# The last quarter of a 256x1024 output closed in two halves on two more PSUM banks

## The reference

```python
h2 = rms_norm(x, ffn_norm_gain)
gate, up = jnp.split(jnp.einsum('bsd,df->bsf', h2, w_gate_up), 2, axis=-1)   # 2816 + 2816 columns
x = x + jnp.einsum('bsf,fd->bsd', jax.nn.silu(gate) * up, w_down)
...
y = x32 * lax.rsqrt(jnp.mean(x32 * x32, axis=-1, keepdims=True) + NORM_EPS)  # the final rms_norm
return (y * gain.astype(jnp.float32)).astype(x.dtype)
```

## Time and profile before

| | |
|---|---|
| median of 3 runs | 873.07 us (872.86 to 874.38) |
| the profiled execution's own time | 873.15 us |
| its span in the trace | 871.3 us |
| TensorE busy | 858.6 us, 99% of the span |
| VectorE busy | 578.6 us, 66% |
| ScalarE busy | 441.0 us, 51% |
| GpSimd busy | 59.8 us, 7% |
| mean granted TensorE clock | 0.998 |

### The profile page before, as it was taken

How to read it: one execution, slowest core, us unless ns; L and a number is a source line. 1 busy time by engine, 2 the same in 40 slices (tenths; PEclk the granted TensorE clock), 3 DMA queues, 4 the chain that set the end, 5 groups by cost and what they waited for, 6 DMA issues and landing times.

```text
span 871.3 us, 13400 instructions
## 1 busy us (share of the span) xinstructions
PE 858.6 (99%) x5434; PEld 742.4 (85%) x5434; DVE 578.6 (66%) x872; ACT 441.0 (51%) x647; POOL 59.8 (7%) x90
## 2 busy tenths in 40 slices
PE   8999999999999999999999999999999999999997
PEld 6888999898899888888889999777888888888885
DVE  5785664654556656565686997876476777877544
ACT  6654434564355544544476652455644555555342
POOL 1000000000020110000020014303000100000000
PEclk9999999999999999999999999999999999999999
DMA  9757754355554555456747783412465665555541
GB/s 291 245 184 217 223 182 139 120 167 179 170 191 156 186 170 169 148 204 204 264 121 253 203 165 107 147 50 50 145 239 161 204 189 177 181 180 192 169 170 48
DMA packets 124771, 151.61 MB, mean 174 GB/s; under 512 B 15991, under 2 KB 87926, under 8 KB 124710
## 3 DMA queue, kind: packets, MB, share of 16 engines
q1 hardware_dynamic: 124426, 150.41, 54.8%
q10 hardware_dynamic: 220, 0.28, 0.1%
q0 software_dynamic: 64, 0.07, 0.0%
HBM read 148.63 MB, written 3.68 MB: 175 GB/s over the span
## 4 chain that ended last, share of the span: by engine, by line
PE 94%; DVE 2%; ACT 1%; SPq 1%; DMA 1%; issue 1%; POOLq 0%; POOL 0%; ACTq 0%; DVEq 0%
PE bank L526 20%; PE bank L528 20%; PE bank L527 20%; PE bank L1345 9%; PE bank L552 5%; PE bank L1346 5%; PE bank L553 3%; PE bank L984 1%; PE bank L744 1%; PE bank L822 1%; PE bank L724 1%; DMA ring<-in_w_in 1%; SPq L1426 1%; PE bank L1106 1%; DVE w_lo L2162 1%
## 5 line engine op out<-in xcount | busy, mean ns | idle before, releaser
L2162 DVE TENSOR_TENSOR w_lo<-ring,w_hi 128x2048 fp32r<-128x2048 f32 (+2 forms) x134 | 297.9, 2228 | 136.6 <-ACT w_hi L1552 136.3
L1552 ACT ACTIVATE w_hi<-ring 128x2048 fp32r<-128x2048 f32 (+2 forms) x134 | 248.9, 1860 | 100.9 <-PE bank L528 74.6
L1345 PE MATMUL bank<-h_both,w_hi 128*128 128x512 f32 x352 | 124.8, 399 | 0.2 <-issue 0.2
L526 PE MATMUL bank<-h_both,w_hi 128*128 128x256 f32 x424 | 122.4, 289 | 0.6 <-DVE w_lo L2162 0.6
L527 PE MATMUL bank<-h_both,w_hi 128*128 128x256 f32 x424 | 119.9, 283 | 0.0
L528 PE MATMUL bank<-h_both,w_lo 128*128 128x256 f32 x424 | 119.9, 283 | 0.0
L1346 PE MATMUL bank<-h_both,w_lo 128*128 128x256 f32 x352 | 98.8, 281 | 0.0
L526 PE MATMUL bank<-w_hi,h_both 128*128 128x512 f32 (+2 forms) x224 | 86.1, 384 | 0.0
L528 PE MATMUL bank<-w_hi,h_both 128*128 128x512 f32 (+2 forms) x224 | 84.1, 375 | 0.0
L527 PE MATMUL bank<-w_lo,h_both 128*128 128x512 f32 (+2 forms) x224 | 84.0, 375 | 0.0
L526 PEld LDWEIGHTS bank<-h_both,w_hi 128*128 128x128 f32 x424 | 81.2, 192 | 2.2 <-issue 1.1
(11 more groups left out here) (407 smaller groups left out, 1517.0 us busy)
## 6 DMA issues: line engine op xcount, KB each, us to landing
ring<-in_w_in SPq DMA_DIRECT2D x59, 1024.0 KB, 5.1
ring<-in_w_gate_up SPq DMA_DIRECT2D x44, 512.0 KB, 4.7
ring<-in_w_down SPq DMA_DIRECT2D x10, 1024.0 KB, 5.0
ring<-in_w_mem_kv SPq DMA_DIRECT2D x8, 1024.0 KB, 9.9
ring<-in_w_gla_out SPq DMA_DIRECT2D x4, 1024.0 KB, 5.0
ring<-in_w_x_out SPq DMA_DIRECT2D x4, 1024.0 KB, 5.3
ring<-in_w_dsa_out SPq DMA_DIRECT2D x4, 1024.0 KB, 5.3
ring<-in_w_o SPq DMA_DIRECT2D x4, 1024.0 KB, 5.0
```

The costliest lines, as they stand in the source:

```text
L526: mm(o, ah, bh, start=start, stop=False, skip_group_check=True)
L1345: mm(o[:, :], wh[:, k - k0, w], h_both[:, :, k, :], start=k == 0, stop=False, skip_group_check=True)
L1552: act(w_hi[:, k % NHI, at:m], ring[:, order.index(name) % NSLOT, at:m], ACT.Copy)\
L2162: tt_(w_lo[:, i, at:m], ring[:, i, at:m], w_hi[:, k % NHI, at:m].bitcast(F), ALU.subtract)\
```

## The change

TensorE now sums only the first 20 of 22 hidden tiles of the last quarter into the bank of `wd11`. The last two tiles are computed as two halves of 256 columns, each in a bank of its own (`wl0`, `wl1`), first all of `wl0` and then all of `wl1`. VectorE adds three banks instead of one to the residual: `wd11` (512 columns, which now holds a partial sum), then `wl0` and `wl1` (256 columns each), and multiplies each half by the gain. ScalarE squares the two halves one after the other into two sums, and GpSimd folds in the extra sum with one more instruction. The last scaling is cut differently: VectorE takes 640 columns and ScalarE 384, where both took 512, and the transfers follow that cut.

```diff
                         q = k // 4
                         if q not in weights:
                             weights[q] = split_unit(f"wd1{q}", 512)
-                        ins = three(o, (f_hi[:, k, s], f_lo[:, k, s]), [w[:, k % 4, :] for w in weights[q]], False, k == FT - 1)
+                        if t == 0 or k < 20:
+                            ins = three(o, (f_hi[:, k, s], f_lo[:, k, s]), [w[:, k % 4, :] for w in weights[q]], False,
+                                        k == (FT - 1 if t == 0 else 19))
                     done(f"wd1{t}", ins)
+                for half in range(2):
+                    bank, part = open_bank(f"wl{half}"), slice(256 * half, 256 * half + 256)
+                    for k in range(20, FT):
+                        ins = three(bank[:, 0:256], (f_hi[:, k, s], f_lo[:, k, s]), [w[:, k % 4, part] for w in weights[5]],
+                                    k == 20, k == FT - 1)
+                    done(f"wl{half}", ins)
...
-                    sp.dma_start(out[0, 128 * t:128 * t + 128, 512 * c:512 * c + 512], xn[:, t, 512 * c:512 * c + 512])\
-                        .then_inc(signal("out_done"), 16)
+                    columns = slice(512 * c, 512 * c + 512 + 128 * t)
+                    sp.dma_start(out[0, 128 * t:128 * t + 128, columns], xn[:, t, columns]).then_inc(signal("out_done"), 16)
...
-                    sc.wait_ge(*read(f"wd{c}{t}"))
-                    half_squares("o", xres[:, t, 512 * c:512 * c + 512], 0, c, t)
-            last = xn[:, 1, 512:1024]
+                    if (c, t) == (1, 1):
+                        sc.wait_ge(*read("wl0"))
+                        act(probT[:, 2, 0:256], xres[:, 1, 512:768], ACT.Square, accum_out=sumsq[:, 8:9])\
+                            .then_inc(signal("sumsq_o"), 1)
+                        sc.wait_ge(*read("wl1"))
+                        act(probT[:, 2, 256:512], xres[:, 1, 768:1024], ACT.Square, accum_out=sumsq[:, 3:4])\
+                            .then_inc(signal("sumsq_o"), 1)
+                    else:
+                        sc.wait_ge(*read(f"wd{c}{t}"))
+                        half_squares("o", xres[:, t, 512 * c:512 * c + 512], 0, c, t)
+            last = xn[:, 1, 640:1024]
             sc.wait_ge(signal("rstd_o"), 2)
-            sc.wait_ge(signal("last_gained"), 1)
+            sc.wait_ge(signal("last_gained"), 2)
...
-                    rsqrt_second(name, col, t, TT + t + 1)
+                    if (name, t) == ("o", 1):
+                        gp.wait_ge(signal("sumsq_o"), 4)
+                        step(nc.gpsimd.tensor_scalar(var[:, 1:2], sumsq[:, 8:9], 1 / D, var[:, 1:2], ALU.mult, ALU.add))
+                    rsqrt_second(name, col, t, TT + t + 1 + (name == "o" and t))
...
+            bank_ready("wd11")
+            stt(xres[:, 1, s], bank_of("wd11")[:, :], rstd[:, 7:8], xres[:, 1, s], ALU.mult, ALU.add).then_inc(reader("wd11"), 1)
+            ve.wait_ge(*read("wd11"))
+            for half in range(2):
+                v = slice(512 + 256 * half, 768 + 256 * half)
+                bank_ready(f"wl{half}")
+                stt(xres[:, 1, v], bank_of(f"wl{half}")[:, 0:256], rstd[:, 7:8], xres[:, 1, v], ALU.mult, ALU.add)\
+                    .then_inc(reader(f"wl{half}"), 1)
+                ve.wait_ge(*read(f"wl{half}"))
+                tt_(xn[:, 1, v], xres[:, 1, v], g_fin[:, v], ALU.mult).then_inc(signal("last_gained"), 1)
+            ve.wait_ge(signal("last_gained"), 2)
+            result(1)
```

More of the change, by code:

```diff
@@ L1992, in _ @@
                 for t in range(TT):
-                    sc.wait_ge(*read(f"wd{c}{t}"))
-                    half_squares("o", xres[:, t, 512 * c:512 * c + 512], 0, c, t)
-            last = xn[:, 1, 512:1024]
+                    if (c, t) == (1, 1):
[9 more added lines that the diff above has]
+            last = xn[:, 1, 640:1024]
             sc.wait_ge(signal("rstd_o"), 2)
-            sc.wait_ge(signal("last_gained"), 1)
+            sc.wait_ge(signal("last_gained"), 2)
             act(last, last, ACT.Copy, scale=rstd[:, 3:4]).then_inc(signal("last_result"), 1)
             sc.wait_ge(signal("last_result"), 1)
-            sc.dma_start(out[0, 128:256, 512:1024], last).then_inc(signal("out_done"), 16)
+            sc.dma_start(out[0, 128:256, 640:1024], last).then_inc(signal("out_done"), 16)
         @block.gpsimd
@@ L2917, in result @@
                 for c in range(2 - t):
-                    o = xn[:, t, 512 * c:512 * c + 512]
+                    o = xn[:, t, 512 * c:512 * c + 512 + 128 * t]
                     tsc(o, o, r, None, ALU.mult).then_inc(signal("result"), 1)
@@ L2923, in _ @@
                 for t in range(TT):
+                    if (c, t) == (1, 1):
+                        break
                     bank_ready(f"wd{c}{t}")
@@ L2928, in _ @@
                     ve.wait_ge(*read(f"wd{c}{t}"))
[L2929 to L2933, removed]
+                    step(tt_(xn[:, t, s], v, g_fin[:, s], ALU.mult))
                     if c == 1:
                         result(t)
+            bank_ready("wd11")
[10 more added lines that the diff above has]
+            result(1)
 def kernel(**inputs):
```

## The result

The changed kernel took 873.88 us (median of 20 runs, 873.17 to 875.66), the kernel before 872.88 (20 runs, 872.13 to 874.38): a ratio of 1.0014, 95% interval 1.0007 to 1.002. That is slower by 1.0 us, inside the 0.2% that I had called no change. The forecast was 873.8.

The account below looks back on a forecast made before the run. TensorE is busy 99% of the span, but the change works only on the 6.2 us relay after its last matmul. Adds +0.89, less what comes back, give +0.7: 873.15 + 0.7 = 873.85, less 0.08 for the median, 873.8 us; range 872.5 to 874.9.

Parts of the forecast that it names:

- VectorE's queue: In the last quarter, VectorE's adds and first gain queue behind the t = 0 scalings; last add ends +0.89 us later.
- the first rival: VectorE keeps up, `wl1`'s add starts when TensorE is done, and transfers start 0.36 us earlier: 872.7 us; chance 0.12.
- TensorE's part: At TensorE's end, twelve 256-column matmuls take 1.43 us instead of 1.36: +0.07 us, costing nothing behind VectorE.
- What comes back: Behind the last add, the narrower square saves 0.22 us; factor +0.67 late, ScalarE's scaling +0.56, VectorE's +0.74.
- the term: The change's whole predicted effect on the kernel's end: +0.7 us.
- The upper bound of 1.0: Top of the bounds on the whole effect, +0.35 to +1.0 us, from the adds and the transfer.
- The estimate of +0.6 from the Trainium skill: Whole effect if VectorE's 256-column steps are priced by (N + 151)/0.96 ns, 0.424 us each: +0.6 us.
- Slow transfers: Final transfers out with mixed row widths run at half rate, +1.5 us on top of +0.7: 875.3 us; chance 0.04.
- The third: Same queue on VectorE, but its cost hidden or halved by overlapping adds or the last gain: +0.2 us, 873.3; chance 0.10.

Follow-up runs that it names:

- e1: The change with three more 256-column matmuls at the end of `wl1`: 873.8 us, ratio 1.0015 to the kernel before.
- e2: The change with the first half's gain moved behind the add of `wl1` on VectorE: 873.33 us, ratio 1.0009 to the kernel before.
- e3: The change with VectorE's scalings of t = 0 moved behind the last gain: 872.99 us, ratio 1.0004 to the kernel before.
- e4: The change with halves over five hidden tiles, VectorE doing partial add, `wl0` add and first gain before the t = 0 scalings: 872.66 us, ratio 0.9997.
- e7: e4 with the last scaling and transfers cut at 512/512 columns: 872.45 us, ratio 0.9994 to the kernel before.
- e6: The kernel before with only the 640/384 cut of the last scaling and transfers: 872.91 us, ratio 0.9999.
- e10: The change run again unaltered (the repetition): 873.65 us, ratio 1.0007 to the kernel before.
- e8: e4 with the cut at 384 columns for VectorE and 640 for ScalarE: 872.69 us, ratio 1.0002 to the kernel before.
- e11: e7 run again unaltered: 872.86 us, ratio 0.9999 to the kernel before.

## Why the prediction was right

**VectorE's queue.** Right, and shown by moving it. Shifting by the 0.17 us that this execution started `wd10`'s add later, I had the adds at 864.82, 865.60 and 866.45, and they started at 864.83, 865.61 and 866.47. e1 (TensorE later: nothing), e2, e3 and e4 (something out of the queue ahead of the last add: it starts earlier by 0.47, 0.82 and 0.98) tell it from TensorE's end and from the new banks. Two figures under the first rival were wrong without touching the sum: VectorE has 1.6 us to do ahead of the last add, and 2.1 only up to its end; and the residual add takes 0.75, the "1.1 us of work" stands in no row.

**TensorE's part.** Twelve matmuls at 0.119, `wl1` full at 865.14 + 0.17 = 865.31; measured 865.33. Its +0.07 (measured 0.08) was hidden, as priced.

**What comes back.** The square: 0.42 instead of 0.63. GpSimd's additional instruction lay at 866.80 to 867.06, under the last square. The scaling: 0.62 instead of 0.72 on ScalarE, 0.55 instead of 0.49 on VectorE. All as worked out. Two handovers weren't, and cancel: the last square starts 0.03 after the add where it was 0.09, and GpSimd starts 0.17 after the sum where it was 0.10. The factor is there 0.7 late, forecast 0.67.

**The sum.** The tail grew by 0.88 (0.82 in the repetition), the term was +0.7, so it was 0.18 too small. 0.04 of that is the choice of 0.7 between 0.74 by the sync engine's issue and 0.56 by ScalarE's: the end followed the sync engine, whose issue moved from 868.24 to 869.24, 0.83 later against the `wd10` add. Most of the 0.09 between 0.74 and 0.83 is VectorE's last scaling, which started 0.10 after GpSimd's factor was written (868.56 to 868.66), where it was 0.04 before; for t = 0 it was 0.10 before as well (863.75 to 863.85), and what decides between the two no run shows. The last 0.05 came behind the issue and is missing in the repetition. The upper bound of 1.0 doesn't follow from its terms: the 1.05 of the adds, less the same 0.15 that brings 0.89 to 0.74, is 0.90. The estimate of +0.6 from the Trainium skill ("VectorE: DVE Perf Modes", section on the TRN2 errata) was further off: the formula agrees with the gain of 256 columns (0.42), but the adds of 256 columns with a per-token factor measured 0.48, not 0.424.

That the forecast of 873.8 came within 0.1 us of 873.88 is partly luck. It starts from 873.07, the median of three runs, and the median of twenty is 872.88; this 0.19 made up for the term's shortfall. The median moved by 1.00; 0.88 is the tail, and the rest is within the scatter.

**The rivals.** That the change does what its words say (-0.4 us) is refuted by the chain and by e1; it becomes true once VectorE has room (e4, e7), where only 0.2 is left of it. Slow transfers are refuted by the window above and e6. The third, that the queue's cost is hidden or halved, is refuted by the timeline: the steps overlap no more than the rows of before showed, and the last add ends 0.91 later (4.76 to 5.67 after the `wd10` add).

Not settled: why this profiled execution starts `wd10`'s add at 861.28, e10's at 861.48 and e2's at 860.37, with the same instructions ahead of it. Nearly all of it is there at the start of the kernel: ScalarE's instruction of L1643 that starts at 56.73 here starts at 56.97 in e10 and at 55.92 in e2. In e6, the kernel before but for the cut, `wd10`'s add even starts at 858.48 (before 861.11), of which 0.54 is there by then (56.06 against 56.60). None of my runs aimed at that; it is why the tail is compared and not the span.

## What to carry to other kernels

Cutting the last tile so that its reader can start early pays only if the reader is free when the first part is ready: write down the reader's program around that point, with the waits in it, before counting what the producer saves. Each piece costs a fixed part (here 0.21 of 0.48 us), and an instruction queued behind an earlier tile's wait doesn't start when its data is there. If there is idle time in the reader, move the cut to where the partial result falls into that idle time; that changed this edit from a loss of 1 us to none that could be measured.

## What the runs showed of the hardware

GpSimd's one-column instruction beside VectorE's two scalings of 512 columns was held in some executions and not in others. It took 0.28 in e4 and 0.59 in e7, e8 and e11, each time started 0.33 to 0.34 us after the scalings had; in e3 another such instruction (L2041), started 0.33 after them, took 0.28. In the two executions in which it wasn't held (e3, e4) the scalings took 0.89 together, in the three others 0.88. Below is e7; the scalings run from 863.85 to 864.73, and it ends 0.05 after them.

```profile
863.85 0.88 DVE L2938 TENSOR_SCALAR arena<-arena 128x512 f32<-128x512 f32 x2
...
864.19 0.59 POOL L2151 TENSOR_SCALAR arena<-arena 128x1 f32<-128x1 f32 x1 [1.02 <-ACT arena L2003]
```

In e4, e7, e8 and e11 it was off the path, and I can't say what decides it.
